# Gate matrix of a product-key expert layer: indexed accumulating transfers in place of one-hot matmuls

## What is computed

```python
q = (t @ wq).reshape(T, PEER_HEADS, 2, PEER_KEY_DIM // 2)        # 8 heads
s1 = einsum('thd,hnd->thn', q[:, :, 0], k1); s2 = einsum('thd,hnd->thn', q[:, :, 1], k2)
v1, i1 = top_k(s1, 16); v2, i2 = top_k(s2, 16)
cand = v1[..., :, None] + v2[..., None, :]                         # 256 pairs
sc, pos = top_k(cand, 16)
idx = take_along_axis(i1 * 128 + i2, pos); g = softmax(sc)
out = sum over h, k of g * gelu(u[idx] . t) * v[idx]
```

## Time and profile before

| | |
|---|---|
| median of 3 runs | 3057.14 us (3055.29 to 3058.13) |
| span of the profiled execution, first to last instruction | 3054.2 us |
| PE busy | 3004.1 us (98%) |
| DVE busy | 2268.2 us (74%) |
| ACT busy | 1409.3 us (46%) |
| POOL busy | 186.1 us (6%) |
| chain that ended last | PE 87%, DVE 9%, ACT 2%, issue 1%, DMA 1% |

### The profile page before, as it was taken

The page is one execution under the profiler, slowest core; times in us unless marked ns, Lnnn a source line. Parts: engine busy times, 40 slices in busy tenths (PEclk is TensorE's granted clock), DMA queues, the critical chain, the costliest instruction groups (busy, mean ns, idle before and its releaser), DMA issues.

```text
span 3054.2 us, 49503 instructions
## 1 busy us (share of the span) xinstructions
PE 3004.1 (98%) x19430; PEld 2799.9 (92%) x19430; DVE 2268.2 (74%) x3252; ACT 1409.3 (46%) x1718; POOL 186.1 (6%) x233
## 2 busy tenths in 40 slices
PE   8999999999999999999999999999999999999998
PEld 8899889999999999999999999999788888888887
DVE  5777559999768988888888877698656646555564
ACT  4464443466445454545454456434445333333333
POOL 1000000020001111111111000000000000000000
PEclk9999999999999999999999999999999999999999
DMA  5443454466668999999999874544444555555554
GB/s 209 178 139 138 157 205 173 166 234 231 237 252 313 358 352 356 351 349 343 359 342 350 317 280 166 194 166 161 157 172 167 185 192 190 191 183 191 192 186 159
DMA packets 102147, 705.59 MB, mean 231 GB/s; under 512 B 13016, under 2 KB 13040, under 8 KB 18464
## 3 DMA queue, kind: packets, MB, share of 16 engines
q1 hardware_dynamic: 78272, 562.07, 50.5%
q0 software_dynamic: 21872, 128.10, 11.9%
q10 hardware_dynamic: 1872, 13.63, 1.1%
HBM read 685.46 MB, written 18.24 MB: 230 GB/s over the span
## 4 chain that ended last, share of the span: by engine, by line
PE 87%; DVE 9%; ACT 2%; issue 1%; DMA 1%; SPq 0%; POOL 0%; POOLq 0%; ACTq 0%; DVEq 0%
PE bank L2018 29%; PE bank L2019 15%; PE bank L2048 7%; PE bank L2050 7%; PE bank L2049 7%; PE bank L1996 6%; PE bank L1997 6%; PE bank L1998 6%; PE bank L2024 2%; DVE raw_lo L1163 2%; DVE split L1163 1%; DVE pick_a L1624 1%; ACT split L713 1%; PE bank L2115 1%; DVE pick_b L1619 1%
## 5 line engine op out<-in xcount | busy, mean ns | idle before, releaser
L2018 PE MATMUL bank<-a_both,split 128*128 128x416 f32 (+1 forms) x3840 | 1222.5, 376 | 2.3 <-DVE split L1163 1.9
L1163 DVE TENSOR_TENSOR raw_lo<-raw,split 128x2048 fp32r<-128x2048 f32 x292 | 668.6, 2290 | 390.2 <-ACT split L713 387.1
L713 ACT ACTIVATE split<-raw 128x2048 fp32r<-128x2048 f32 x308 | 588.6, 1911 | 487.8 <-DMA raw<-stream_dram 308.1
L2018 PEld LDWEIGHTS bank<-a_both,split 128*128 128x128 f32 x3840 | 721.1, 188 | 55.8 <-issue 5.9
L2019 PE MATMUL bank<-a_both,split 128*128 128x208 f32 x3072 | 762.0, 258 | 0.0
L2019 PEld LDWEIGHTS bank<-a_both,split 128*128 128x128 f32 x3072 | 584.6, 190 | 0.9
L1996 PE MATMUL bank<-a_both,split 128*128 128x256 f32 (+1 forms) x1984 | 572.5, 289 | 12.0 <-DVE raw_lo L1163 6.8
L1163 DVE TENSOR_TENSOR split<-raw,split 128x2048 fp32r<-128x2048 f32 x240 | 549.6, 2290 | 33.0 <-ACT split L713 11.0
L729 ACT ACTIVATE split<-raw 128x1536 fp32r<-128x1536 f32 x224 | 333.8, 1490 | 505.3 <-PE bank L2019 501.3
L1997 PE MATMUL bank<-a_both,split 128*128 128x256 f32 (+1 forms) x1984 | 560.4, 282 | 0.0
L1998 PE MATMUL bank<-a_both,raw_lo 128*128 128x256 f32 (+1 forms) x1728 | 488.8, 283 | 0.0
(11 more groups left out here) (344 smaller groups left out, 3071.0 us busy)
## 6 DMA issues: line engine op xcount, KB each, us to landing
raw<-stream_dram SPq DMA_DIRECT2D x532, 1024.0 KB
gates_scratch<-stage ACTq DMA_DIRECT2D x13, 1024.0 KB, 4.3
gbuf<-gates_scratch POOLq DMA_DIRECT2D x30, 416.0 KB, 6.9
x<-x_dram SPq DMA_DIRECT2D x4, 512.0 KB, 7.1
x_scratch<-x POOLq DMA_DIRECT2D x1, 2048.0 KB, 11.4
mem<-mem_dram POOLq DMA_DIRECT2D x1, 2048.0 KB, 9.5
xm<-x_scratch POOLq DMA_DIRECT2D x1, 2048.0 KB, 12.1
out_dram<-x SPq DMA_DIRECT2D x4, 512.0 KB, 3.0
```

Source lines behind the costliest of these rows:

```text
L713: eng.activation(high(k, is_near(k))[:, :], raw[:, k % RAW, :], ACT.Copy).then_inc(hi_done, 1)
L1163: eng.tensor_tensor(low(k, is_near(k)), raw[:, k % RAW, :], high(k, is_near(k))[:, :].bitcast(F32), ALU.subtract).then_inc(split_done, 1)
L2018: mm(o, hi[:, ks], pair, start=kt == 0, stop=False)
```

## The change

The gate matrix is not multiplied out any more. It lies in DRAM as `gates_scratch`, one number for each place. POOL fills it with zeros ahead of time, in 13 transfers of 1 MB during `v1` and `z`. Then, head by head, each pick's place is computed as an offset (`slots_of`), its gate as a number (`gates_for`), and POOL adds the 128 gates of one pick column to their places with one indirect accumulating transfer (L650 of the changed kernel): 16 for the second tile, and for the first tile's 80 dense tokens the 80 x 16 offsets and gates are written to DRAM and read back as 128 x 10, so that 10 transfers do. That is 26 for each head and 208 in all. POOL waits for the preceding head's adds before the next head's, and for all before it loads `gbuf` for round 0. On DVE the heads are finished one at a time, with the splits of 39 units written between the pieces (`SPLIT_BEHIND`); ACT takes the exponentials of a head right behind a split (`EXP_AFTER`), now with gelu before and after in `u0` and `u1`. The key scores move into a unit (behind its matmul group 4), and `u1` is no longer "near". The diff, cut to its core:

```diff
+        gates_d = nc.dram_tensor("gates_scratch", (P * GATE_ROW, 1), F32, kind="Internal").ap()
+        gates_rows = gates_d.rearrange("(p n) one -> p (n one)", p=P)
+        near_d = nc.dram_tensor("near_scratch", (PEER_HEADS, 2, FAR, TOPK), U32, kind="Internal").ap()
...
+        SPLIT_BEHIND = {}
+        _k = 3
+        for _h, _counts in enumerate([(1, 1, 1, 0, 2, 0), (1, 0, 1, 1, 1, 0), (1, 0, 1, 1, 1, 0), (1, 1, 1, 0, 1, 1),
+                                      (1, 1, 1, 0, 2, 0), (1, 1, 1, 1, 1, 0), (1, 1, 1, 1, 1, 0), (2, 1, 1, 0, 2, 0)]):
+            for _piece, _n in enumerate(_counts):
+                if (_h, _piece) == (0, 0):
+                    _k += 1
+                SPLIT_BEHIND[_h, _piece] = [_k + i for i in range(_n)]
+                _k += _n
+        PICK_UNITS = 48
+        ZERO_PARTS = GATE_ROW // 2048
+        assert GATE_ROW == ZERO_PARTS * 2048
+        EXP_AFTER = {SPLIT_BEHIND[h, 4][0] - 3: h for h in range(PEER_HEADS)}
...
+        NEAR0, NEAR1 = UNIT0["e0"], UNIT0["ck"]
...
+        KEYS_AT = {2 * h + 2: h for h in range(PEER_HEADS)}
+        KEYS_KT = 4
...
+                if h == 8:
+                    for n in range(ZERO_PARTS):
+                        eng.wait_ge(mm_done, UNIT0["v1"] + n + 1)
+                        cs = slice(n * 2048, n * 2048 + 2048)
+                        eng.dma_start(gates_rows[:, cs].rearrange("p (a b) -> p a b", b=256),
+                                      zeros[:, :].unsqueeze(1).to_broadcast([P, 8, 256])).then_inc(s_zeros, 16)
...
+            def add_picks(tt, h, picks):
+                for k in picks:
+                    if tt == 1:
+                        c = TOPK * h + k
+                        idx, src = offs[:, 1, 0, c:c + 1], offs[:, 1, 1, c:c + 1].bitcast(F32)
+                    else:
+                        idx, src = near_offs[:, h, 0, k:k + 1], near_offs[:, h, 1, k:k + 1].bitcast(F32)
+                    eng.indirect_dma_start(gates_d, bass.IndirectOffsetOnAxis(ap=idx, axis=0), src, None,
+                                           compute_op=ALU.add).then_inc(s_added[tt], 16)
+            eng.wait_ge(s_zeros, 16 * ZERO_PARTS)
+            for h in range(PEER_HEADS):
+                eng.wait_ge(picks_ready, h + 1)
+                eng.dma_start(near_d[h, :, :, :].rearrange("a p k -> p a k"), offs[G:P, 0, :, TOPK * h:TOPK * h + TOPK])\
+                    .then_inc(s_near_out, 16)
+                eng.wait_ge(s_added[1], 16 * TOPK * h)
+                add_picks(1, h, range(0, TOPK // 2))
+                eng.wait_ge(s_near_out, 16 * (h + 1))
+                eng.dma_start(near_offs[:, h, :, :], near_d[h, :, :, :].rearrange("a p k -> a (p k)")
+                              .rearrange("a (q j) -> q a j", j=NEAR_PICKS)).then_inc(s_near, 16)
+                add_picks(1, h, range(TOPK // 2, TOPK))
+                eng.wait_ge(s_near, 16 * (h + 1))
+                eng.wait_ge(s_added[0], 16 * NEAR_PICKS * h)
+                add_picks(0, h, range(NEAR_PICKS))
...
+            eng.wait_ge(s_added[1], 16 * PICKS)
+            eng.wait_ge(s_added[0], 16 * NEAR_PICKS * PEER_HEADS)
+            for g in range(4):
+                load_gates(0, g)
             eng.wait_ge(idx_done, 1)
...
+            def gate_exp(h):
+                eng.wait_ge(sm_dve, h + 1)
+                for tt in range(TT):
+                    eng.activation(sc[:, tt, h, :], sc[:, tt, h, :], ACT.Exp, bias=nfirst[:, h, tt:tt + 1],
+                                   accum_out=gsum[:, h, tt:tt + 1]).then_inc(sm_act, 1)
...
+                eng.wait_ge(mm_done, UNIT0["wq"] + s + 1)
                 if s < 16:
-                    eng.wait_ge(mm_done, UNIT0["wq"] + s + 1)
                     eng.activation(qT[:, s, :], bank[s % 4][:, 0:T], ACT.Copy).then_inc(bank_free, 1)
-                    ahead(UNIT0["wq"] + s)
-            def gelu0(g, j):
-                eng.activation(act0[:, g * 4 + j, 0:TD], bank[j][:, 0:TD], ACT.Gelu).then_inc(bank_free, 1)
-            eng.wait_ge(s_xw, 16)
-            def gate_exp(k):
-                if k in (8, 12):
-                    tt = (k - 8) // 4
-                    eng.wait_ge(sm_dve, tt + 1)
-                    eng.activation(sc[:, tt, :, :], sc[:, tt, :, :], ACT.Exp).then_inc(sm_act, 1)
-            feature("u0", 16, 0, gelu0, unroll=True, between=gate_exp)
-            def evict_group(q):
-                block, half = q // 4, (q // 4) % 2
-                if q % 4 == 0 and block >= 2:
-                    eng.wait_ge(g_write[half], 16 * (block // 2))
-                eng.wait_ge(g_mm, 4 * q + 4)
-                eng.activation(stage[:, half, :, 4 * (q % 4):4 * (q % 4) + 4].rearrange("p n t -> p t n"),
-                               bank[4 + q % 4][:, :].rearrange("p (t n) -> p t n", t=4), ACT.Copy).then_inc(g_evict, 1)
-                if q % 4 == 3:
-                    eng.wait_ge(g_evict, q + 1)
-                    eng.dma_start(gates_d[block, :, :], stage[:, half, :, :].rearrange("p n t -> p (n t)"))\
-                        .then_inc(g_write[half], 16)
-                    eng.activation(gbuf[:, 0:2, block:block + 1, :].rearrange("p g b n -> p (g b) n"),
-                                   stage[:, half, 0:8, :].rearrange("p (g n) t -> p g (n t)", g=2), ACT.Copy)\
-                        .then_inc(g_early, 1)
-            for k in range(16):
-                u, groups = UNIT0["u1"] + k, GATES_UNIT.get(k, [])
-                for q in groups[:4]:
-                    evict_group(q)
-                eng.wait_ge(mm_done, u + 1)
-                eng.activation(act1[:, k, 0:TD], bank[k % 4][:, 0:TD], ACT.Gelu).then_inc(bank_free, 1)
-                ahead(u)
-                for q in groups[4:]:
-                    evict_group(q)
+                elif s < 32:
+                    if s == 16:
+                        eng.wait_ge(s_xw, 16)
+                    eng.activation(act0[:, s - 16, 0:TD], bank[s % 4][:, 0:TD], ACT.Gelu).then_inc(bank_free, 1)
+                else:
+                    eng.activation(act1[:, s - 32, 0:TD], bank[s % 4][:, 0:TD], ACT.Gelu).then_inc(bank_free, 1)
+                ahead(UNIT0["wq"] + s)
+                if s in EXP_AFTER:
+                    gate_exp(EXP_AFTER[s])
...
-            def evict_group(q):
-                block, half = q // 4, (q // 4) % 2
-                if q % 4 == 0 and block >= 2:
-                    eng.wait_ge(g_write[half], 16 * (block // 2))
-                eng.wait_ge(g_mm, 4 * q + 4)
-                eng.activation(stage[:, half, :, 4 * (q % 4):4 * (q % 4) + 4].rearrange("p n t -> p t n"),
-                               bank[4 + q % 4][:, :].rearrange("p (t n) -> p t n", t=4), ACT.Copy).then_inc(g_evict, 1)
-                if q % 4 == 3:
-                    eng.wait_ge(g_evict, q + 1)
-                    eng.dma_start(gates_d[block, :, :], stage[:, half, :, :].rearrange("p n t -> p (n t)"))\
-                        .then_inc(g_write[half], 16)
-                    eng.activation(gbuf[:, 0:2, block:block + 1, :].rearrange("p g b n -> p (g b) n"),
-                                   stage[:, half, 0:8, :].rearrange("p (g n) t -> p g (n t)", g=2), ACT.Copy)\
-                        .then_inc(g_early, 1)
...
+            def slots_of(h):
+                hs = slice(TOPK * h, TOPK * h + TOPK)
+                eng.tensor_scalar(nfirst[:, h, :], sc[:, :, h, 0], -1.0, None, ALU.mult).then_inc(sm_dve, 1)
+                own.did(eng.tensor_tensor(key_x[:, :, :, :], top_i[:, :, 2 * h:2 * h + 2, :],
+                                          slot_x[:, :].unsqueeze(1).unsqueeze(1).to_broadcast([P, TT, 2, TOPK]), ALU.bitwise_or))
+                own.did(eng.tensor_scalar(posab[:, 0, :, :], pos[:, :, h, :], 4, 7, ALU.logical_shift_right, ALU.logical_shift_left))
+                own.did(eng.tensor_scalar(posab[:, 1, :, :], pos[:, :, h, :], 15, 7, ALU.bitwise_and, ALU.logical_shift_left))
+                own.wait()
+                for half in range(2):
+                    own.did(eng.tensor_tensor(differ[:, half, :, :, :],
+                                              posab[:, half, :, :].unsqueeze(3).to_broadcast([P, TT, TOPK, TOPK]),
+                                              key_x[:, :, half, :].unsqueeze(2).to_broadcast([P, TT, TOPK, TOPK]),
+                                              ALU.bitwise_xor))
+                own.wait()
+                for half in range(2):
+                    own.did(eng.tensor_reduce(key_at[:, half, :, hs], differ[:, half, :, :, :], AX.X, ALU.min))
+                own.wait()
+                own.do(eng.scalar_tensor_tensor(row_off[:, :, :], key_at[:, 0, :, hs], float(TD),
+                                                C("tok").unsqueeze(2).to_broadcast([P, TT, TOPK]), ALU.mult, ALU.add))
+                own.do(eng.scalar_tensor_tensor(offs[:, :, 0, hs], key_at[:, 1, :, hs], float(GATE_ROW), row_off[:, :, :],
+                                                ALU.mult, ALU.add))
+            def gates_for(h):
```

(98 more changed lines are left out.)

213 lines of the change are left out of this document (58 added, 155 removed).

## The result

The changed kernel takes **3234.2 us** (median of 4 runs, 3231.7 to 3236.6) where the kernel before takes 3057.6 in the same comparison: a ratio of 1.0574, 95% interval 1.0559 to 1.0589. The profiled execution has a span of 3229.0 us, 174.8 more than before. The prediction had the sign but only a third of the size: +62 us, and its range ended at 3145.

What follows compares the result with a forecast made beforehand. PE, busy 98%, was taken as the bound; removal frees 70.5 us, but POOL's adds end unit 0 of `e0` 57 us later, plus 2 clock and 3 layouts: +62, span 3116, plus 2.9, 3119 us; range 2988 to 3145.

Steps and rivals of the forecast that it cites:

- The removal: In `u0` and `u1`, without gate groups, split waits and lower clock: units of 5.36 us, `u1` ending at 701.4, not 771.9.
- VectorE's room: From first key scores to end of `u1`: heads 112 us plus splits 108 us, 220 in about 255 us available.
- The zeros: 13.6 MB written in some 75 us at 182 GB/s: costs nothing, or a few us if loads are delayed.
- The pitch of a free add: On POOL with nothing interfering: 1.24 us per add, from a gather's 0.94 and 0.30 between two gathers.
- The pitch beside splits: On POOL from 471 to 701: three adds per 5.36 us unit, 1.79 us each, so 126 adds.
- the exclusion: POOL cannot read its indices while VectorE runs a two-SBUF-input instruction such as a split, leaving 3.1 us free per unit.
- From the last add to unit 0 of `e0`: Before `e0`: landing, load of `gbuf`, four gatings and PE's last tiles take 27 us after the last add is issued.
- Behind unit 0: After unit 0 of `e0`: 2 us for the lower clock and 3 us for layouts ahead of the `act1` loads.
- Hidden adds: Rival: POOL keeps up at a pitch of about 1.0 us, last add at 689; 2989 to 3000 us, chance 0.30.
- Adds far dearer: Rival: adds at 2.5 us and more each, last at 991, kernel far over 3200 us; chance 0.10.
- the main case: Adds beside splits at a mean pitch of 1.5 to 1.9 us: 3090 to 3140 us, chance 0.42.
- the upper bound: Price of one add on POOL: nothing excludes that an add, which must read its target, takes twice a gather.

## Why the prediction was right in sign and wrong in size

- **The removal.** Units of 5.36 us and no wait of TensorE for a split in `wq`, `u0`, `u1`: as predicted. That `u1` ends at 701.6 and so within 0.2 us of 701.4 is in part luck: in the kernels with fewer adds or none, alike up to there, `wq` begins up to 4 us later and `u1` ends at up to 706.0. VectorE's room and ScalarE's were judged rightly. The zeros cost little: in the 75 us in which they go out TensorE is busy for 73.7, against 74.4 before.
- **The pitch of a free add: the step that failed.** The prediction says "So 1.24 us when nothing interferes", from a gather of 0.94 and a pause of 0.30. The pause is right; the add takes 1.55, so 1.85, and the 0.59 between an add and the same transfer without addition is what the sum left out. Against the kernel without addition, 208 x 0.59 is 123 us; 8 of them come back, since at a slower pace fewer transfers meet a split (their excess over the free duration is 61 us there, 53 here), and 2 because the first add begins sooner. That makes the 113 us between 809.1 and 922.0, nearly all of the 115 by which the last add is later than the 807 of the prediction.
- **The pitch beside splits.** 1.79 us predicted, 2.48 measured (91 steps from 473.6 to 699.2), 92 adds by the end of `u1` instead of 126. Without the addition it is 127 at 1.79: the exclusion was counted rightly. The other 116 adds took 220 us, 1.91 each with the direct transfers between them, where the prediction had 82 in 102.
- **From the last add to unit 0 of `e0`**: 27 us predicted, 23.9 measured. The terms as written (1.2, 6.9, 14.7, 1.2 and 2) make 26.0; 27 needs the add's own 0.94 as well. Measured are 3.6 for the add and its landing, 3.7 for the load of `gbuf` in place of 8.1, and 16.6 from the first gating to the end of unit 0. The lower clock is in it: when TensorE starts again after 230 us of standing, the granted clock is 0.50, the level of 1.2 GHz, as the last window shown above has it.
- **Behind unit 0**: 5.6 us measured, 5 predicted in two terms. 1.4 of it is unit 1, which ends 6.3 us behind unit 0 instead of 4.9, 2.2 a wait for a split near 1170; the rest is at the end of the kernel. So the 5 were right in total, in part by luck: the prediction put its 3 down to the layouts, and the wait seen is one for a split.
- **The rivals.** Hidden adds would have given 2989 to 3000; without adds it is 3004, and 2994 with the gates weighed sooner. The rival's price was near; its condition, a pitch of 1.0, is far off. "Adds far dearer" was priced from 2.5 us a piece: the measured mean is 2.17 (207 steps from 473.6 to 922.0), between it and the main case's 1.9.
- **The range.** The prediction wrote down the upper bound itself ("takes twice a gather") and did not carry it to the end: 1.88 and 0.30 are 2.18 a piece free, more than the 1.85 that was measured. By that the last add is past 920 and the kernel past 3230. The range stopped at 3145 because the main case's pitch ended at 1.9, only 0.11 over the count for a gather, which allowed the unknown instruction next to nothing.

What stays open: where in the instruction the 0.59 us of the addition go. Halving the elements of an add saved 0.15 us, so the elements account for at most 0.30 and at least 0.29 are fixed, if the second half costs what the first does; the transfer without addition was not run with 64 partitions. The pages show more packets, and nothing here looks inside the instruction. A version was not built that makes the adds few (the repacked 80, with the way through DRAM covered) and leaves the second tile to one-hot tiles.

## What to carry to other kernels

When a sum is one unmeasured price times 208, the range is that price's bounds times 208: take a value between them, not the nearest relative's. Ask of a transfer chain what it costs per instruction on the issuing engine, since 64 elements instead of 128 made a tenth of difference, and hold count times price against the stretch that is to hide it: 208 x 1.85 = 385 us never fitted into 230. If such a chain must run beside VectorE, cut VectorE's long instructions: it was worth 44 us here, in one run.

## What the runs showed of the hardware

- An indexed transfer with addition keeps POOL for 1.55 us (1.40 with 64 partitions), without it for 0.96, as a read of single elements for 0.945. Where POOL waits for nothing else, the gap between two of them is 0.29 to 0.31 us in all eight kernels that have them.
- An add on 128 partitions sends 144 packets, on 64 partitions 80, and the same transfer without addition 32.
- An add that starts inside a split of VectorE (two inputs, 2.29 us) needs 1.41 to 1.49 us from the split's end on; one that had started 0.28 us ahead of it is not touched (1.54 us). Beside the 1.23 us `tensor_scalar` both are held. Inside a `TENSOR_REDUCE` an add is not (1.55 us).
- Direct transfers of POOL lie over the end of the add in front of them (one begins at 700.34 in the kernel with 80 adds, 0.57 us before the add of 699.36 ends); no two indexed ones overlap in any of the traces.
